# Expert rows gathered by blocks of eight tokens and summed in four column groups, in a two-layer transformer block

## The reference

```
q  = (h @ w_q) as 8 heads of 2 x 128                  # per token
s1, s2 = q_first @ keys1.T, q_second @ keys2.T        # 128 scores each
v1, i1 = top_k(s1, 16);  v2, i2 = top_k(s2, 16)
sv, si = top_k(v1 + v2 as 256 pairs, 16)              # 16 experts per head
idx = i1[si // 16] * 128 + i2[si % 16]
g = softmax(sv)
a = gelu(sum_d u_tab[idx] * h)                        # 16 rows of 1024 per head
y = sum over heads and slots of (g * a) * v_tab[idx]  # again 16 rows per head
x = x + gate * y
```

## Time and profile before

| | |
|---|---|
| median of 3 runs | 2988.36 us |
| lowest, highest | 2987.4, 2995.51 us |
| span of the profiled execution | 3175.8 us |
| mean granted TensorE clock | 0.902 |
| PE busy | 2281.8 us (72%) |
| DVE busy | 1622.6 us (51%) |
| POOL busy | 1709.2 us (54%) |
| ACT busy | 608.3 us (19%) |
| moved by DMA | 918.09 MB, mean 289 GB/s |

### The profile page before, as it was taken

How to read it: one execution, slowest core, us unless ns; L and a number is a source line. 1 busy time by engine, 2 the same in 40 slices (tenths; PEclk the granted TensorE clock), 3 DMA queues, 4 the chain that set the end, 5 groups by cost and what they waited for, 6 DMA issues and landing times.

```text
span 3175.8 us, 26554 instructions
## 1 busy us (share of the span) xinstructions
PE 2281.8 (72%) x7694; PEld 1174.7 (37%) x7694; DVE 1622.6 (51%) x3941; ACT 608.3 (19%) x1356; POOL 1709.2 (54%) x1642
## 2 busy tenths in 40 slices
PE   6989547767786687776767767687876765547767
PEld 4768212333352344332243322346762222212222
DVE  1245764555574555654446644434376445565433
ACT  2141111122211121111111211124211111111111
POOL 0000757646647656567655577540046776656774
PEclk8999879988899999899888899889988998879998
DMA  9523969968869988999979999970358998888996
GB/s 304 194 67 106 333 224 360 348 229 293 313 242 372 331 310 303 359 348 337 345 288 330 316 360 375 348 275 27 102 205 295 362 364 307 302 305 307 354 370 251
DMA packets 329368, 918.09 MB, mean 289 GB/s; under 512 B 27408, under 2 KB 131616, under 8 KB 329120
## 3 DMA queue, kind: packets, MB, share of 16 engines
q0 software_dynamic: 221184, 805.40, 68.6%
q1 hardware_dynamic: 108064, 111.24, 10.8%
HBM read 915.49 MB, written 1.05 MB: 289 GB/s over the span
## 4 chain that ended last, share of the span: by engine, by line
PE 29%; issue 16%; POOL 15%; DMA 14%; DVE 12%; another core or an unknown queue 10%; ACT 2%; SPq 0%; POOLq 0%; DVEq 0%; ACTq 0%
POOL RING L511 15%; PE acc L1086 14%; DMA RING<-in_p_v,IV 10%; PE wk L1147 4%; PE wk L1267 3%; PE wk L1280 2%; DMA WR<-in_ada_w 2%; DMA RING<-in_p_u,IU 2%; DVE TI L600 1%; ACT SCR L996 1%; DVE STM L772 1%; PE wk L1115 1%; PE wk L1076 1%; DVE RING L611 1%
## 5 line engine op out<-in xcount | busy, mean ns | idle before, releaser
L1086 PE MATMUL acc<-RING,DG 128*128 128x512 f32 x3072 | 1511.5, 633 | 623.4 <-DMA RING<-in_p_v,IV 325.1
L611 DVE SCALAR_TENSOR_TENSOR RING<-RING,H 128x1024 f32<-128x1024 f32 x768 | 922.3, 1224 | 767.7 <-DMA RING<-in_p_u,IU 724.0
L511 POOL DMA_INDIRECT RING<-in_p_u,IU x768 | 830.0, 1081 | 661.8 <-DVE RING L611 227.6
L1086 PEld LDWEIGHTS acc<-RING,DG 128*128 128x128 f32 x3072 | 570.4, 198 | 1552.5 <-issue 1155.8
L511 POOL DMA_INDIRECT RING<-in_p_v,IV x768 | 855.0, 1113 | 292.1 <-issue 203.7
L919 ACT ACTIVATE DG<-ident,WT 128x128 f32<-128x128 f32 x768 | 294.1, 399 | 1272.9 <-PE acc L1086 882.6
L508 POOL COPY IU<-IDX 128x16 uint32<-128x16 uint32 (+1 forms) x48 | 15.1, 314 | 488.2 <-DVE WG L874 488.0
L619 DVE TENSOR_TENSOR acc<-acc,BC 128x1024 f32<-128x1024 f32 x48 | 59.1, 1232 | 187.2 <-PE acc L1086 96.9
L1280 PE MATMUL wk<-HT,WR 128*128 128x256 f32 x576 | 132.5, 387 | 13.6 <-issue 11.8
L1147 PE MATMUL wk<-WR,HT 128*128 128x256 f32 x448 | 107.7, 397 | 34.2 <-ACT HT L947 20.3
L1280 PEld LDWEIGHTS wk<-HT,WR 128*128 128x128 f32 x576 | 110.8, 194 | 33.0 <-issue 16.4
(11 more groups left out here) (160 smaller groups left out, 1726.1 us busy)
## 6 DMA issues: line engine op xcount, KB each, us to landing
WR<-in_ada_w SPq DMA_DIRECT2D x34, 1024.0 KB
WR<-in_p_w_q SPq DMA_DIRECT2D x18, 1024.0 KB
RING<-in_ada_w SPq DMA_DIRECT2D x14, 1024.0 KB, 11.9
RING<-in_p_u,IU POOLq DMA_INDIRECT x768
RING<-in_p_v,IV POOLq DMA_INDIRECT x768
WR<-in_o_w_in SPq DMA_DIRECT2D x8, 1024.0 KB
RING<-in_p_w_q SPq DMA_DIRECT2D x6, 1024.0 KB, 11.2
WR<-in_e_w_in SPq DMA_DIRECT2D x5, 1024.0 KB
```

Of the source, the lines that this page charges most:

```text
L511: pool.indirect_dma_start(out=ring[:, n % NU, :], out_offset=None, in_=tables[table], in_offset=bass.IndirectOffsetOnAxis(ap=rows, axis=0) ...
L611: nc.vector.scalar_tensor_tensor(out=U[:, s % NU, :], in0=U[:, s % NU, :], scalar=1.0, in1=H[:, tile, :], op0=ALU.mult, op1=ALU.mult, accu ...
L1086: ins = nc.tensor.matmul(acc[:, par, hf * 512:hf * 512 + 512], DG[:, s % 4, :], V[:, s % NV, hf * 512:hf * 512 + 512], start=(s == 0), sto ...
```

## The change

1. **V rows by blocks.** A gather into V brings for 8 tokens all their 16 slots, 128 rows as before, instead of one slot of 128 tokens. The indices for it must be turned: VectorE writes the chosen indices once more, spread with a mask M8 (IE, `expand`), TensorE multiplies them with a selector S16 ("ixT", two matmuls of 16 columns for each topk), VectorE copies the result to IDV.
2. **Sums in column groups.** The partition of V is now (token of 8, slot of 16). A matmul sums over it: its weights are 128x32 with 8 columns that are not zero, and it writes 32 rows of PSUM. The four gathers of a step are four column groups, `acc[32 * g:32 * g + 32]`. The weights (ST) come once per chunk: VectorE spreads the weights with M8 (WE), TensorE multiplies with a selector SELW (one 128x512 matmul, stage "weights"), ScalarE copies to ST. The 16 diagonals per chunk are gone. TensorE waits for all four v slots of a step, then issues eight matmuls; the slots are released by the last four.
3. **Accumulation over a tile.** PSUM sums over all eight heads of a tile; `update` runs once per tile, in the second chunk of the next.
4. **Unrolled loops.** All chunks are written out, each in four steps of four slots: GpSimd issues four u and four v gathers in turn, VectorE has four dots, TensorE four slots of the chunk before. GpSimd reads indices straight from IDX and IDV; its copies and two semaphore increments are gone.
5. **Stages between steps.** The topk is in three parts, each behind another step; attention comes in pieces of two units, and the other stages stand one by one behind steps (`spread`).
6. Buffers and small moves: buffers T1 and DG gone, PL and PW moved, the rotary embedding written with one temporary less, the pool weights loaded by two DMAs.

The core of the diff:

```diff
+def choosing(l):
+
+    f = {}
+    for t in TILES[l]:
+        for h, tile, q in ((1, t, 2), (3, t, 3), (5, t + 1, 0), (7, t + 1, 1)):
+            if tile in TILES[l]:
+                for part in range(3):
+                    f[t, h, part] = [("topk", l, tile, q, part)]
+                f[t, h, 3] = [("ixT", l, tile, q)]
+    return f
+
+
+def spread(f, lo, hi, items):
+
+    steps = [(t, h, q) for t in range(4) for h in range(PH) for q in range(4) if lo <= (t, h, q) <= hi]
+    for i, item in enumerate(items):
+        f.setdefault(steps[i * len(steps) // len(items)], []).append(item)
...
+    spread(f, (1, 0, 0), (1, 2, 3), [("bc", 0, CTX, (G1, SC2)), ("bc", 0, CTX, (SH2, G2)), ("out", 0, CTX), ("norm", 0, 2, CTX),
+                                     ("hT", 0, 2, CTX), ("rows", 0, CTX), ("score", 0, CTX, (0, 1)), ("score", 0, CTX, (2, 3))])
...
+            def gather_u(c, s):
+                if c > 0 or s >= NU:
+                    pool.wait_ge(dotted, c * TOPK + s - NU + 1)
+                col = (c % PH) * TOPK + s
+                gather("u", U, s, IDX[:, (c // PH) % 2, col:col + 1], u_in)
+
+            def gather_v(c, s):
+                if c > 0 or s >= NV:
+                    pool.wait_ge(vsum, c * TOPK + s - NV + 1)
+                col = (c % PH) * TOPK + s
+                gather("v", V, s, IDV[:, (c // PH) % 2, col:col + 1], v_in)
+
+            def turned(l, c):
+                tile, h = (c - chunk0(l, 0)) // PH, c % PH
+                pool.wait_ge(*evac(("ixT", l, tile, h // 2)))
...
+            def update(l, tile):
+
+                n = chunk0(l, tile) // PH
                 g2 = G2B[tile // 2]
-                dve.wait_ge(vsum, (c + 1) * TOPK)
-                nc.vector.tensor_tensor(acc[:, par, :], acc[:, par, :], g2, ALU.mult).then_inc(updated, 1)
-                dve.wait_ge(updated, 2 * c + 1)
-                nc.vector.tensor_tensor(X[:, tile, :], X[:, tile, :], acc[:, par, :], ALU.add).then_inc(updated, 1)
-
-            def chunk(l, tile, p, hh, vtile, start):
-                c = chunk0(l, tile) + 2 * p + hh
-                dots(c, hh, tile)
-                dve.wait_ge(gelud, c + 1)
-                col = (2 * p + hh) * TOPK
-                g = WG[:, tile % 2, col:col + TOPK] if isinstance(p, int) else WG[:, tile % 2, bass.ds(col, TOPK)]
-                nc.vector.tensor_tensor(WT[:, hh, :], GA[:, hh, :], g, ALU.mult).then_inc(weighted, 1)
-                if not start:
-                    update(c - 1, 1 - hh, vtile)
+                dve.wait_ge(vsum, (n + 1) * PH * TOPK)
+                nc.vector.tensor_tensor(acc[:, n % 2, :], acc[:, n % 2, :], g2, ALU.mult).then_inc(updated, 1)
+                dve.wait_ge(updated, 2 * n + 1)
+                nc.vector.tensor_tensor(X[:, tile, :], X[:, tile, :], acc[:, n % 2, :], ALU.add).then_inc(updated, 1)
+                last[0] = (updated, 2 * n + 2)
+
+            def expand(out, rows, nh):
+
+                return nc.vector.tensor_tensor(out.rearrange("p h (j k) -> p h j k", j=8),
+                                               rows.unsqueeze(2).to_broadcast([P, nh, 8, TOPK]),
+                                               M8[:, :].unsqueeze(1).unsqueeze(3).to_broadcast([P, nh, 8, TOPK]), ALU.mult)
...
+            def vsums(c, q):
+
+                n, h = c // PH, c % PH
+                if q == 0:
+                    pe.wait_ge(*evac(("wT", c)))
+                if (h, q) == (0, 0) and n > 1:
+                    pe.wait_ge(updated, 2 * n - 2)
+                for s in range(4 * q, 4 * q + 4):
                     pe.wait_ge(v_in[s % NV], 16 * (2 * c + s // NV + 1))
-                    pe.wait_ge(diag, c * TOPK + s + 1)
-                    for hf in range(2):
-                        ins = nc.tensor.matmul(acc[:, par, hf * 512:hf * 512 + 512], DG[:, s % 4, :],
+                for hf in range(2):
+                    for g in range(4):
+                        s = 4 * q + g
+                        ins = nc.tensor.matmul(acc[32 * g:32 * g + 32, n % 2, hf * 512:hf * 512 + 512], ST[:, c % 2, s, :],
                                                V[:, s % NV, hf * 512:hf * 512 + 512],
-                                               start=(s == 0), stop=(s == TOPK - 1))
-                    ins.then_inc(vsum, 1)
+                                               start=((h, q) == (0, 0)), stop=((h, q) == (PH - 1, 3)))
+                        if hf == 1:
+                            ins.then_inc(vsum, 1)
...
+                elif kind == "ixT":
+                    _, l, tile, q = s
+                    pe.wait_ge(chosen.sem, chosen.at("topk", l, tile, q))
+                    o = begin(s)
+                    for hh in range(2):
+                        ins = nc.tensor.matmul(o[:, hh * TOPK:(hh + 1) * TOPK], IE[:, q % 2, hh, :], S16[:, :], start=True, stop=True)
+                    done(ins)
+                elif kind == "weights":
+                    c = chunk0(s[1], s[2]) + s[3]
+                    pe.wait_ge(weighted, c + 1)
+                    o = begin(("wT", c))
+                    done(nc.tensor.matmul(o, WE[:, c % 2, :], SELW[:, :, :].rearrange("p s n -> p (s n)"), start=True, stop=True))
```

More of the change, by code:

```diff
@@ L515, in chunk @@
-            def chunk(l, tile, p, hh, vtile, vcol, first):
-                c = chunk0(l, tile) + 2 * p + hh
-                start = first and hh == 0 and tile == 0
-                static = isinstance(p, int)
-                if not (static and c < 2):
-                    gate(issued, 32 * c - 48)
-                col = (2 * p + hh) * TOPK
-                copy_rows(IU[:, hh, :], tile, slice(col, col + TOPK) if static else bass.ds(col, TOPK))
-                if not start:
-                    copy_rows(IV[:, 1 - hh, :], vtile, vcol)
-                gate(ixcopy, 2 * c + 1)
-                for s in range(TOPK):
-                    if not (static and c == 0 and s < NU):
-                        gate(dotted, c * TOPK + s - NU + 1)
-                    gather("u", U, s, IU[:, hh, s:s + 1], u_in)
-                    if not start:
-                        if not (static and c == 1 and s < NV):
-                            gate(vsum, (c - 1) * TOPK + s - NV + 1)
-                        gather("v", V, s, IV[:, 1 - hh, s:s + 1], v_in)
+                                        in_offset=bass.IndirectOffsetOnAxis(ap=rows, axis=0)).then_inc(slot_in[n % NU], 16)
@@ L605, in topk16, with dots @@
                         after()
-            def dots(c, hh, tile):
-                for s in range(TOPK):
+            def dots(c, q, tile):
+                for s in range(4 * q, 4 * q + 4):
                     dve.wait_ge(u_in[s % NU], 16 * (2 * c + s // NU + 1))
@@ L650, in _ @@
                 elif kind == "tables":
-                    dve.wait_ge(loaded["small"], 96)
+                    dve.wait_ge(loaded["small"], 112)
                     for tt in range(2):
```

358 lines of the change are left out of this document (164 added, 194 removed).

## The result

The changed kernel takes **2860.3 us** (median of 4 runs, 2857.9 to 2865.2) beside 2990.2 us for the kernel before (4 runs, 2987.4 to 2995.5): a ratio of 0.956, 95% interval 0.953 to 0.959. It is faster by 130 us. The forecast was 2660 us with a range of 2570 to 2790, so the gain is under half of the one forecast. The profiled run took 2861.0 us at a span of 2859.2.

A forecast was written before the change was run, and what follows sets the result against it. The prediction took transfers to bound the gather stages, with stalls removable. 493.5 us outside them, 2281 of transfers, 34 starts and ends and 30 blocks made 2839 us of span, converted to 2660 us; range 2570 to 2790.

The forecast's parts named there:

- the conversion: Whole kernel: summed span of 2839 us turned into device time, 2672 in proportion or 2652 less 187 us; 2660 taken.
- The sum: Whole span: 493.5 us outside gather stages, 2281 transfers at 375 GB/s, 34 starts and ends, 30 blocks: 2839 us.
- the second failed step: GpSimd's gathers: some taking 1.64 us were read as full queues, with transfers setting the pace, not GpSimd.
- VectorE's wait for u rows: Sign in the profile after: u rows stay VectorE's largest wait, with more than the 724 us before.
- Topk in three parts: VectorE in gather stages: holds of 23.7 us become parts of 5 to 8 us between steps; their stalls go entirely.
- V sums, diagonals: TensorE: four v slots take 1.9 to 3.8 us instead of 6.9; 294 us of ScalarE copies go; nothing saved directly.
- GpSimd: Gather issue: two index copies per chunk go; plain gathers stay 1.24 us each, 2.48 per slot, below transfers' 2.8.
- Start: Start of each gather stage: GpSimd idle 11.58 us, unchanged, and 5 us at the end: 17 per layer, 34.
- Stages between steps: Blocks on TensorE: output projection loses 12 us, four score pairs 3 each, 6 elsewhere: 30 us, bounds 0 and 180.
- Half clock: Rival: TensorE falls to 1.2 GHz, long blocks double and lose 105 us in place of 24; 2740 us; chance 0.14.
- Cover too short: Rival: each of some 45 filled steps loses 4 us, 180 in place of 30; 2810 us; chance 0.11.
- TensorE starved of instructions: Rival: instruction supply at 0.92 us per TensorE record makes a step 14.7 us; slower, 3540 us; chance 0.04.

The follow-up runs named there:

- Experiment 1: The kernel before, with no edit, run and profiled once more: 2991.7 us, ratio 1.000 to itself, profile span 3002.7 us.
- Experiments 5 and 6: Changed kernel with dots over 512 of 1024 columns: 2746.5 us; changed kernel with half of each v row transferred: 2894.0 us.
- experiment 3: Changed kernel with the old v layout (one token per partition, ScalarE diagonals, full-width matmuls): 2876.1 us, ratio 0.959 to the kernel before.
- experiment 7: Kernel of Experiment 4 with the old v layout, diagonals and full-width matmuls: 2819.1 us, ratio 0.943 to the kernel before.
- Experiment 4: Changed kernel with stages in smaller pieces and the first tile's second topk moved behind the first steps: 2810.5 us, ratio 0.941 to the kernel before.
- the halves: Kernel of Experiment 4 with each dot product made as two 512-column instructions, nothing left out: 2741.7 us beside 2820.6 on a quiet chip.
- experiments 12 and 11: On one disturbed chip: 12 is the halves, 2894.5 us; 11 is the kernel of Experiment 4, 2902.0 us; the kernel before 3182.9 us.

## Why the forecast was wrong

**The step that failed first is the conversion**: "Taken in proportion (x 0.941) the sum gives 2672, taken as the same 187 us 2652." The sum itself was 2839 us of span, with 1610 and 740 us for the two gather stages; the span is 2859.2, with 1606.0 and 756.5. The 187 us between profile and median were taken as a price of profiling that stays. Experiment 1 shows the kernel before with a profile of 3002.7 us, so they were stalls of that one execution, and they lay in the gather stages. The sum replaced those stages by bytes at an undisturbed rate, so it had taken the stalls out already; the conversion took them out a second time. Without it the forecast would have been 2841, 0.7% off. (The upper end of the forecast's own range has a slip besides: 2876 and 40 us more are 2916, in proportion 2744 and not 2710.)

**That closeness is partly luck**, and the second failed step says why: "That a gather now and then takes 1.64 us inside the instruction I read as full queues: transfers set the pace there, not GpSimd." Experiments 5 and 6 refute it. The rate of 375 GB/s was no property of the transfers but GpSimd's pace with its stretches, and it happened to hold in the changed kernel (366 and 355). On the kind of chip that the rows came from, the changed kernel takes 2950 us where the sum has 2841: 109 us too little, with 353 and 342 GB/s between the first and the last gather. One of the forecast's signs said so: VectorE's wait for u rows was to grow beyond 724 us, as it would under a bound of transfers, and it is 629.1 us.

*Topk in three parts*: right in kind, "Its stalls go entirely" was too much. The split is worth 45 us. On a quiet chip the stall before was smaller than in the earlier trace rows, where 7.68 us of it were the remote waits, which the forecast put down to an instruction stream; no row names such a source.

*V sums, diagonals*: right that a step costs nothing by itself, with 1.92 us for 16 records at full clock and 3.64 at half, inside the bounds of 1.9 to 3.8; the groups overlap. The catching up, for which TensorE was to be relieved, is worth 16 us, not clear of noise (experiment 3), and nothing that can be measured once blocks are short (experiment 7). TensorE, after:

```profile
1882.42 1.92 PE L1081 MATMUL acc<-RING,ST 128*32 128x512 f32 x16 [0.69 <-ACT ST L1042]
1891.42 3.64 PE L1081 MATMUL acc<-RING,ST 128*32 128x512 f32 x16 [7.08 <-DMA RING<-in_p_v,IDV]
```

*GpSimd*: the floor of 2.48 us a slot was right, and the index copies that go were worth more than a word. In experiment 1's trace a v gather ends at 2775.81 and the next gather starts at 2777.13 with two copies between, 1.32 us in place of 0.30. Over the 48 chunks of that trace the time above 0.30 us adds up to 54 us, in the term that bounds the kernel. The forecast gave it no term in its sum; no run puts the copies back into the changed kernel, so what they are worth there is not shown.

*Start*: "GpSimd idle 11.58 us, unchanged" was wrong: 25.16 and 25.37 us, since the change puts VectorE's copy of `ixT` ahead of the first dots, behind scores on TensorE. *Stages between steps*: 12 us for the output projection became a wait of 20.46, and the attention pieces, counted among "the rest", took up to 9.49 us each. Experiment 4 won 50 us from start and blocks together; the sum had 34 + 30 for them.

*Rivals.* Half clock: the granted clock is 0.68 and 0.63 in the gather stages, the lower level of 1.2 GHz in part, as that rival had it, but the long output projection ran at full clock (27.57 us for 127 records), and the old layout at a granted clock of 0.96 (experiment 3) is no faster; its 2740 is not what was measured. Cover too short forecast 2810 by waits at the blocks; GpSimd's waits for dots and v slots are only 164 us in all, less than the 335 before. TensorE starved of instructions did not occur. What sets the pace, GpSimd held by dots, was in none of them.

*What stays open*: how the 130 us divide (45 are the split topk; unrolling, the index copies, the fewer updates and the stages between steps were not taken apart), what the remote waits are (the trace names no source) and whether they belong to a chip or to a session, and why the halves gain 79 us on one kind of chip and 7 to 9 on the other; there the waits for dots were 209 us with the halves and 133 without, and GpSimd's remote waits 101 and 32 us (experiments 12 and 11), but no run takes these away.

## What to carry to other kernels

Before a profile is scaled to another time, look for waits in it that no instruction of the program releases, and ask whether the sum has already removed them. A high DMA share with a busy issuing engine does not tell which of the two is the bound: divide the busy time of the issuing engine by its instructions, compare with its shortest instruction, and lay the two engines' timelines side by side where they differ. Where VectorE runs beside GpSimd's gathers, count its long instructions with two SBUF inputs. Here cutting such an instruction in two, more work in total, gained 79 us on a quiet chip, where taking 57% off TensorE's v sums gave 16 by the medians.

## What was not expected of the hardware

An indirect gather that starts during a VectorE instruction with two SBUF inputs, a dot product or a topk's product, not at its very start or end, ends 0.80 to 0.82 us after it (442 of 442 in the changed kernel); during an update, with one input in PSUM, it is not held (0 of 88). Alone it takes 0.94 us, and 0.30 us pass between two. Rows of half the size (2 KB in place of 4 KB) do not shorten the gather (0.95 us). The transfers reached 410 GB/s over 130 us, above the 395 that the forecast had as its upper end. The same program took 2987 to 2992 us in some sessions and 3165 to 3183 in others, each on its own chip, and 2860 or 2950 after the change, so a change's worth differs with them: 4.4% and 7.4%.
